# Two weight slots taken per arriving tile of rows in four places, and the key norms' root moved forward

## What is computed

```python
# layer 0: FFN 0, RWKV-7 time mixing, FFN 1; layer 1: FFN 2, short gated convolution, FFN 3
x = x + 0.5 * swiglu(rms(x), w_gu, w_down)         # w_gu 1024 x 5632, w_down 2816 x 1024
r, k, v = xr @ w_r, xk @ w_k, xv @ w_v             # xr, xk, ...: mixtures of a row and the one before
w = decay of (tanh(xw @ w1) @ w2); a = sigmoid(a0 + (xa @ a1) @ a2)
kk = k * k_k, divided per head by max(norm(kk), 1e-12)      # "the key norms"
x = x + o @ w_o                                     # "wo"; o from the recurrence over the tokens
b, c, u = split(rms(x) @ w_in); x = x + (b * conv(c * u)) @ w_out      # "scin", "scout"
```

## Time and profile before

| | |
|---|---|
| median of 3 runs | 1481.89 us (1480.38 to 1483.07) |
| the profiled execution | 1481.93 us, of which the span of the trace is 1480.1 us |
| TensorE busy | 1402.2 us (95%) |
| VectorE, ScalarE, GpSimd busy | 853.8, 584.7, 22.8 us |
| share of the chain that ended last | PE 87%, DVE 5%, ACT 4% |
| granted TensorE clock, mean over the span | 0.965 of full speed |

### The profile page before, as it was taken

One profiled execution on the slowest core, in us unless ns is written; L12 is line 12 of the kernel. 1 busy time (PEld: TensorE's weight loads), 2 busy tenths in 40 slices (PEclk: granted clock), 3 DMA queues, 4 the chain that ended last, 5 costly groups with the idle time before them and its releaser, 6 DMA issues.

```text
span 1480.1 us, 28445 instructions
## 1 busy us (share of the span) xinstructions
PE 1402.2 (95%) x11742; PEld 1359.1 (92%) x11742; DVE 853.8 (58%) x1275; ACT 584.7 (40%) x754; POOL 22.8 (2%) x36
## 2 busy tenths in 40 slices
PE   4999999697799999899999999999999999999997
PEld 4999999586689996699999999999999999999997
DVE  4555544776868254665555455555546766555543
ACT  5333333476344331354333334433333235433332
POOL 0000000300000000200000000000000000000000
PEclk9999999898799797799999999999999999999999
DMA  4433334232135111034433444443444444434342
GB/s 193 151 140 138 137 131 155 86 116 85 60 84 187 36 48 53 29 131 154 142 142 126 147 162 150 154 142 124 139 157 149 147 143 140 167 143 142 128 155 96
DMA packets 44219, 188.97 MB, mean 128 GB/s; under 512 B 15888, under 2 KB 17296, under 8 KB 28016
## 3 DMA queue, kind: packets, MB, share of 16 engines
q1 hardware_dynamic: 44144, 187.89, 36.9%
HBM read 182.65 MB, written 5.22 MB: 127 GB/s over the span
## 4 chain that ended last, share of the span: by engine, by line
PE 87%; DVE 5%; ACT 4%; issue 2%; POOL 1%; DMA 1%; SPq 0%; ACTq 0%; DVEq 0%
PE psum L330 46%; PE psum L362 21%; PE psum L804 5%; PE psum L498 4%; ACT w_hi L243 2%; PE psum L1032 1%; DVE w_lo L248 1%; PE psum L983 1%; PE psum L1052 1%; PE psum L830 1%; PE psum L1001 1%; PE psum L958 1%; PE psum L876 1%; DMA w_raw<-in_gu 1%; PE psum L1048 1%
## 5 line engine op out<-in xcount | busy, mean ns | idle before, releaser
L330 PE MATMUL psum<-x_hi,w_hi 128*128 128x322 f32 (+2 forms) x1600 | 501.4, 313 | 23.5 <-DVE x_lo L295 17.8
L248 DVE TENSOR_TENSOR w_lo<-w_raw,w_hi 128x2048 fp32r<-128x2048 f32 (+1 forms) x188 | 388.2, 2065 | 226.3 <-ACT w_hi L243 225.9
L243 ACT ACTIVATE w_hi<-w_raw 128x2048 fp32r<-128x2048 f32 (+1 forms) x188 | 325.8, 1733 | 459.3 <-PE psum L330 227.2
L330 PE MATMUL psum<-x_lo,w_hi 128*128 128x322 f32 (+2 forms) x1600 | 500.8, 313 | 0.0
L330 PE MATMUL psum<-x_hi,w_lo 128*128 128x322 f32 (+2 forms) x1600 | 499.4, 312 | 0.0
L330 PEld LDWEIGHTS psum<-x_hi,w_hi 128*128 128x128 f32 x1600 | 302.2, 189 | 26.4 <-issue 22.7
L330 PEld LDWEIGHTS psum<-x_hi,w_lo 128*128 128x128 f32 x1600 | 302.9, 189 | 0.0
L330 PEld LDWEIGHTS psum<-x_lo,w_hi 128*128 128x128 f32 x1600 | 302.7, 189 | 0.3
L362 PE MATMUL psum<-h_hi,w_hi 128*128 128x322 f32 (+2 forms) x704 | 219.5, 312 | 0.0
L362 PE MATMUL psum<-h_lo,w_hi 128*128 128x322 f32 (+2 forms) x704 | 219.4, 312 | 0.0
L362 PE MATMUL psum<-h_hi,w_lo 128*128 128x322 f32 (+2 forms) x704 | 219.2, 311 | 0.0
(11 more groups left out here) (200 smaller groups left out, 1394.2 us busy)
## 6 DMA issues: line engine op xcount, KB each, us to landing
w_raw<-in_gu SPq DMA_DIRECT2D x88, 1024.0 KB, 4.7
w_raw<-in_down SPq DMA_DIRECT2D x64, 704.0 KB, 4.1
w_raw<-in_mix SPq DMA_DIRECT2D x16, 1024.0 KB, 4.7
w_raw<-in_scin SPq DMA_DIRECT2D x12, 1024.0 KB, 4.8
w_raw<-in_wo SPq DMA_DIRECT2D x4, 1024.0 KB, 5.5
w_raw<-in_scout SPq DMA_DIRECT2D x4, 1024.0 KB, 4.7
s<-in_wkv SPq DMA_DIRECT2D x8, 256.0 KB, 3.4
out_wkvs<-s SPq DMA_DIRECT2D x8, 256.0 KB, 2.0
```

The costliest lines, as they stand in the source:

```text
L243: act.activation(whi[par][:, :tiles * P], raw[par][:, :tiles * P], ACT.Copy).then_inc(hi_ready, 1)
L248: dve.tensor_tensor(wlo[par][:, :n], raw[par][:, :n], whi[par][:, :n].bitcast(F32), ALU.subtract).then_inc(lo_ready, 1)
L330: last = pe.matmul(PS[:, banks[j], :n], w[:, (2 * k + j) * P:(2 * k + j + 1) * P], v[:, k, :n], start=(k == 0 and i == 0), stop=(k == KT - ...
```

## The change

1. `dual(lag)` orders the tiles of two slots: tile k of slot 0, and from step `lag` on also tile k - lag of slot 1 behind it. It is used in the first feed-forward block (lag 2), for the key projection in the time mixing, and for wo and scout (lag 3 each). The product of one tile moves to `pe_tile`. With lag 2 slot 0 ends after 13 of the 16 tiles, with lag 3 after 12 of 16; before, after 8.
2. In the first feed-forward block `norm_pe` comes after 14 of the 16 tiles.
3. In `project_pe` the waits for the weights of both slots 0 and 1 stand ahead of the first product.
4. In all four feed-forward blocks VectorE makes the `w_lo` that slot 2 needs ahead of the wait for `rstd`, not behind lines 422 and 423.
5. The key norms' bound, root and reciprocal move forward. 
6. Ahead of two of the seven norms (the time mixing's, the final one) ScalarE does an Ln on one column of a constant.

```diff
         def norm_act(act, norm, n):
+            if norm in (1, 6):
+                act.activation(spare[:, 0:1], con[:, K_ONES:K_ONES + 1], ACT.Ln)
             act.wait_ge(ss_done, norm + 1)
...
+        def dual(lag):
+
+            for step in range(KT + lag):
+                if step < KT:
+                    yield 0, step
+                if step >= lag:
+                    yield 1, step - lag
+
+        def pe_tile(pe, par, banks, k, n, xh, xl, shift=0):
+            for j in range(2):
+                for i, (w, v) in enumerate(passes(whi[par], wlo[par], xh, xl)):
+                    last = pe.matmul(PS[:, banks[j], shift:shift + n], w[:, (2 * k + j) * P:(2 * k + j + 1) * P], v[:, k, :n],
+                                     start=(k == 0 and i == 0), stop=(k == KT - 1 and i == 2))
+            return last
...
-            gu_slot(0, 0, fresh=True)
-            norm_pe(pe, {0: 0, 1: 2, 2: 3, 3: 5}[f], 0, n)
-            gu_slot(0, 1)
+            if f == 0:
+                pe_slot_wait(pe, gu)
+                pe.wait_ge(scaled, d["scaled"] + 2)
+                for par, k in dual(2):
+                    if par == 0:
+                        pe.wait_ge(xlo_ready, 8 * d["ver"] + k + 1)
+                    elif k == 0:
+                        pe_slot_wait(pe, gu + 1)
+                    elif k == KT - 2:
+                        norm_pe(pe, 0, 0, n)
+                    last = pe_tile(pe, par, (2 * par, 2 * par + 1), k, n, xhi, xlo)
+                    if k == KT - 1:
+                        last.then_inc(slot_used, 1)
+            else:
+                gu_slot(0, 0, fresh=True)
...
                 if first:
+                    split_dve(dve, gu // 2 + i + 1, par, tiles)
                     norm_dve(dve, {0: 0, 1: 2, 2: 3, 3: 5}[f], n)
...
-                split_dve(dve, gu // 2 + i + 1, par, tiles)
+                if not first:
+                    split_dve(dve, gu // 2 + i + 1, par, tiles)
...
+            pe.wait_ge(scaled, SCALED_BEFORE[name])
+            if name == "wo":
+                pe.wait_ge(mix_evac, MIX_GROUPS - 4)
+            for s in range(2):
                 pe_slot_wait(pe, first + s)
                 pe.wait_ge(x_new, 8 * q + 2 * s - 2)
+            for s, k in dual(3):
                 if s == 0:
...
-            for s in range(4):
-                project(s, XK, s == 0, s == 3, PAD)
+            pe_slot_wait(pe, MIXB)
+            banks = [open_group(), open_group()]
+            for par, k in dual(3):
...
+            act.wait_ge(kk_max, 1)
+            act.activation(tmp[3][0:HEADS, :T], tmp[3][0:HEADS, :T], ACT.Sqrt).then_inc(kk_root, 1)
...
-                if s == 1:
-                    act.wait_ge(kk_max, 1)
-                    act.activation(tmp[3][0:HEADS, :T], tmp[3][0:HEADS, :T], ACT.Sqrt).then_inc(kk_root, 1)
...
+                if k == 3:
+                    dve.wait_ge(kk_root, 1)
+                    dve.reciprocal(rstd[0:HEADS, :], tmp[3][0:HEADS, :T]).then_inc(kk_inv, 1)
...
-            dve.wait_ge(kk_root, 1)
-            dve.reciprocal(rstd[0:HEADS, :], tmp[3][0:HEADS, :T]).then_inc(kk_inv, 1)
```

More of the change, by code:

```diff
@@ L107, in build_program @@
         con = at("con", [P, NCONST])
+        spare = at("spare", [P, 8])
         cin = at("cin", [P, KT * 2 * SEQS])
@@ L345, in ffn_pe @@
                 pe.wait_ge(x_new, 8 * (2 if f == 1 else 5) + 6)
-            gu_slot(0, 0, fresh=True)
-            norm_pe(pe, {0: 0, 1: 2, 2: 3, 3: 5}[f], 0, n)
-            gu_slot(0, 1)
+            if f == 0:
[13 more added lines that the diff above has]
+                gu_slot(0, 0, fresh=True)
+                norm_pe(pe, {0: 0, 1: 2, 2: 3, 3: 5}[f], 0, n)
+                gu_slot(0, 1)
             with pe.Fori(1, FT // 2) as i:
@@ L484, in project_pe @@
             first = stream[name][0]
-            for s in range(4):
+            pe.wait_ge(scaled, SCALED_BEFORE[name])
+            if name == "wo":
+                pe.wait_ge(mix_evac, MIX_GROUPS - 4)
+            for s in range(2):
                 pe_slot_wait(pe, first + s)
                 pe.wait_ge(x_new, 8 * q + 2 * s - 2)
+            for s, k in dual(3):
                 if s == 0:
-                    pe.wait_ge(scaled, SCALED_BEFORE[name])
-                    if name == "wo":
-                        pe.wait_ge(mix_evac, MIX_GROUPS - 4)
+                    pe.wait_ge(olo_ready, olo_base + k + 1)
+                last = pe_tile(pe, s, (2 * s, 2 * s + 1), k, n, ohi, olo)
+                if k == KT - 1:
+                    last.then_inc(slot_used, 1)
+            for s in range(2, 4):
+                pe_slot_wait(pe, first + s)
+                pe.wait_ge(x_new, 8 * q + 2 * s - 2)
                 banks = ((2 * s) % 4, (2 * s + 1) % 4)
                 for k in range(KT):
[L494 to L499, removed]
+                    last = pe_tile(pe, s % 2, banks, k, n, ohi, olo)
                 last.then_inc(slot_used, 1)
@@ L832, in lora_out @@
                     last.then_inc(mix_out, 1)
-            for s in range(4):
-                project(s, XK, s == 0, s == 3, PAD)
+            pe_slot_wait(pe, MIXB)
+            banks = [open_group(), open_group()]
+            for par, k in dual(3):
+                if par == 0:
+                    pe.wait_ge(xlo_ready, 8 * XK + k + 1)
+                elif k == 0:
+                    pe_slot_wait(pe, MIXB + 1)
+                last = pe_tile(pe, par, (banks[par], banks[par] + 1), k, T, xhi, xlo, PAD)
+                if k == KT - 1:
+                    last.then_inc(mix_out, 1)
+            for s in range(2, 4):
+                project(s, XK, False, s == 3, PAD)
             lora_inner(4, XW)
@@ L1421, in mix_dve @@
                 low(XA, k)
+            dve.wait_ge(kk_ss, PAIRS)
+            dve.tensor_scalar(tmp[3][0:HEADS, :T], PS[0:HEADS, 6, :T], 1e-24, None, ALU.max).then_inc(kk_max, 1)
             dve.memset(ar[:, 1, :, 0:PAD], 0.0)
@@ L1432, in mix_dve @@
                     lora_low(1, 1)
-            dve.wait_ge(kk_ss, PAIRS)
-            dve.tensor_scalar(tmp[3][0:HEADS, :T], PS[0:HEADS, 6, :T], 1e-24, None, ALU.max).then_inc(kk_max, 1)
+                if k == 3:
+                    dve.wait_ge(kk_root, 1)
+                    dve.reciprocal(rstd[0:HEADS, :], tmp[3][0:HEADS, :T]).then_inc(kk_inv, 1)
             split(6)
-            dve.wait_ge(kk_root, 1)
-            dve.reciprocal(rstd[0:HEADS, :], tmp[3][0:HEADS, :T]).then_inc(kk_inv, 1)
             split(7)
```

## The result

| | before | changed kernel |
|---|---|---|
| median | 1481.89 us (1480.38 to 1483.18, 5 runs) | 1490.43 us (1485.55 to 1496.71, 5 runs) |
| ratio to before | | 1.0061, 95% interval 1.0038 to 1.0084 |
| the profiled execution | 1481.93 us, span 1480.1 | 1485.55 us, span 1483.8 |
| mean granted TensorE clock of it | 0.965 | 0.963 |

The changed kernel is 0.6% slower, against a forecast of 1488.7 us (+0.46%). The profiled execution was the fastest of its five, so its trace shows only 3.7 us of the 8.5. A second execution (the last experiment) took 1493.42 us.

What follows compares the result with a forecast made beforehand. TensorE, busy 95% of the span, bounds the kernel, so edits count mainly by its waits. +1.65 - 3.7 - 0.7 + 0.1 - 0.75 + 2.1 + 5.3 + 2.8 = +6.8 us gives 1488.7 us, range 1483.0 to 1491.5.

Steps and rivals of the forecast that it cites:

- First block: First feed-forward block: slot 0 ends later, so slot 2 starts at 38.8 instead of 37.15 us, +1.65 us.
- Blocks 2 to 4: Feed-forward blocks two to four: w_lo no longer holds slot 2, which can follow slot 1 at once, together -3.7 us.
- Keys: Key projection in the time mixing: row waits filled, slot 2 held for w_lo, starting at 297.3 against 298.19, -0.9 us.
- Extra Ln: Time mixing's norm and last norm: loads no table earlier, only adds an activation, +0.2 and +0.1 us.
- Key norms: Time mixing: ScalarE 1.3 us ahead, about a quarter of the 2.24 us reciprocal exposed, -0.75 us.
- wo: Output projection wo: no row waits to fill, slot 0 ends later and slot 2 waits until 629.6, +2.1 us.
- scout: Output projection scout: first waits for slot 1's w_lo, 3.1 us, then slot 2 starts at 1226.8, together +5.3 us.
- Clock: First block and scout: long new waits drop TensorE to half clock, 1.4 us each, +2.8; nothing for wo and scout's slot 2 holds.
- more clock: Rival: the holds in wo and scout also let the clock fall, +3.4 us, 1492.1 us; chance 0.1.
- Releases partly hidden: Rival: releases partly hidden, or reciprocal not exposed and keys' slot 2 not held, clock up, 1484.4 us; chance 0.15.
- Faster: Rival: TensorE holds the loop over pairs, so VectorE's 12.0 us of w_hi waits could go, 1477.5 us; chance 0.05.
- Clock stays up: Rival: holds as walked, but clock stays up in the first block and at scout, +4.0 us, 1485.9 us; chance 0.2.

Runs made afterwards that it cites:

- experiment 12: The changed kernel unchanged, measured again as a second set of runs with a second profiled execution: 1487.00 us, ratio 1.0047, +7.0 us.
- experiments 7: The changed kernel with wo and scout put back to the order of before: 1477.33 us, ratio 0.9975, -3.7 us.
- Experiment 4: The changed kernel with the wait for slot 1's weights in wo and scout moved to ahead of slot 1's first tile: 1484.12 us, ratio 1.0019.
- experiment 2: The kernel before with only w_lo made ahead of the wait for rstd in all four feed-forward blocks: 1475.91 us, ratio 0.9963, -5.5 us.
- experiment 6: The kernel before with only the key projection in the new order of slots 0 and 1: 1480.26 us, ratio 0.9993.
- experiment 11: The kernel before with only the extra Ln ahead of the time mixing's norm and the final one: 1480.17 us, ratio 1.0.
- experiment 3: The kernel before with only the key norms' bound, root and reciprocal moved forward: 1480.47 us, ratio 0.9992.
- experiment 9: The kernel before with the new order of slots 0 and 1 in scout only: 1489.54 us, ratio 1.0077, +11.4 us.
- 10: The kernel before with the new order of slots 0 and 1 in wo only: 1485.67 us, ratio 1.0045, +6.7 us.
- experiment 1: The kernel before with the new order of slots 0 and 1 in wo and scout only: 1493.22 us, ratio 1.0069, +10.2 us.

## Why the prediction was right

The forecast of +6.8 us stands just below the two measurements by ratio, +9.0 (5.6 to 12.4) and +7.0 (3.4 to 10.5), and inside both intervals. The time, 1490.43 us, fell in its range, near the upper end. By its own steps:

- **First block, +1.65.** Slot 2 at 38.8 was forecast. It came at 38.30 (+1.15) and 38.93 (+1.78), and at 38.41 and 37.70 in experiments 7 and 4, released by the multiplication by `rstd`, as forecast.
- **Blocks 2 to 4, -3.7.** Slot 2 comes 14.92, 14.83 and 14.84 us after its block's start, where it was 16.12, 16.13 and 15.97: -3.6. The one wait for `w_lo` that is left is scin's. The stages as a whole gained 3.2 us, in experiment 2 without the extra Ln 4.0; the last section has what I know of this difference.
- **Keys, -0.9**: -0.9 (experiment 6, and 18.49 after the first product in the changed kernel). **Extra Ln, +0.2 and +0.1**: 0.11 us at the time mixing's norm and nothing at the last one (experiment 11), and no table load moved.
- **Key norms, -0.75**: -0.9 against the one trace of before, -0.7 against the mean of seven (experiment 3). About a quarter of the reciprocal was to be exposed, 0.56 us. ScalarE waits 0.81 us for the row behind it where it waited 0.34 us before, 0.5 us more.
- **wo, +2.1.** The changed kernel's trace shows only +1.0 (32.42 against 31.39), which would make the term half wrong. The clock hides the rest. The projection starts in a stretch at half clock, and that stretch lasted 6.0 us into wo in the trace of before and 3.4 in the one of after. Two pairs of executions with the same clock from the start of wo to slot 2: 3.5 us at half in experiment 9, where wo is unchanged, gives 15.96 us, and 3.4 in the changed kernel gives 18.04; 6.0 before gives 17.10, and 6.1 in experiment 12 gives 19.23. Both pairs differ by **2.1 us**.
- **scout, +5.3**, 3.1 of them ahead of the first product. That wait cost 3.4 (TensorE starts 5.00 us after scin, not 1.62). From the first product to slot 2 it is 17.60 instead of 14.11, +3.5. The sum, with what the clock takes there, is 6.9; 5.3 + 1.4 = 6.7 was forecast. Experiment 4 takes the first wait away, and the stretch at half clock with it: by the ratios 6.2 us (4.2 against the second set). From the end of scin to block 4 its trace is 3.3 us shorter than that of the changed kernel, although the clock fell behind its hold.
- **Clock, +2.8**, for one stretch each in the first block and at scout. Both are there in both traces of the changed kernel, and the sum counts them about rightly (+0.8 us from slot 2 of the first block to the time mixing, or +1.5 against experiment 11; 1.4 of the 3.5 us in scout). This is still the term that was mis-sized. "So there I count nothing", the prediction said of the 2 us holds in wo and scout. It had set a wait of 2.0 us, behind which the clock fell, against a hold of 1.9 us in scin, behind which it didn't. In the trace of before they read, with a third one that it passed over:

```profile
329.18 0.42 PE L830 MATMUL psum<-t_hi,w_hi 128*128 128x336 f32 x1 [1.86 <-ACT sw L1131]
336.99 0.42 PE L830 MATMUL psum<-t_hi,w_hi 128*128 128x336 f32 x1 [2.23 <-ACT bk L1131]
1134.35 0.42 PE L330 MATMUL psum<-x_hi,w_hi 128*128 128x322 f32 x1 [1.56 <-DVE w_lo L248]
```

The clock fell behind the wait of 1.86 us (at 329.73) and stayed up behind the longer one of 2.23 us (until 343.38). So waits of about 2 us had gone both ways already, and half a chance for each new hold was nearer than none. In the changed kernels the clock fell behind 4 of 10 such holds (scout in experiments 4 and 9, wo in 10 and 12; not in experiment 1, nor in the first trace of after). From slot 2 to the end wo then takes 15.88 instead of 14.38 us, scout 15.7 instead of 14.1: 1.5 each. Two holds at 0.4 chance make 1.2 us. So the rival *more clock* was no rival but a part of the forecast that comes and goes, and moves an execution of the changed kernel by 1.5 or 3 us. That this widens its spread is not shown: it is 11.2 and 10.0 us in its two sets, and up to 10.8 us in those of the kernel before.
- **Rivals.** *Releases partly hidden* fell: all four waits are there, the keys' slot 2 is held by 0.7 us, and a part of the reciprocal is exposed. *Faster* fell: TensorE does not hold the loop over pairs, where VectorE's wait for `w_hi` grew to 14.4 us though TensorE's key slots ended earlier. *Clock stays up* fell with the two stretches.

With the terms as measured the sum is some +7.4 us (first block +1.2, blocks 2 to 4 -3.2, keys with the extra Ln -0.8, norms -0.8, wo +2.1, scout with its clock +6.9, clock in the first block +0.8, behind the two holds +1.2), and no term is off by more than 1.2 us. The total is not right by large errors that cancel.

Two things stay open. By the ratios scout alone (+11.4) and wo alone (+6.7) add up to 18 us, and both together gave 10.2 us, which is apart by more than the intervals. By the medians it is 9.1 + 5.3 = 14.4 against 12.1 us, and that the runs don't tell apart. The stages of the traces allow 9 us without and 13 us with all falls of the clock. What makes wo alone larger than its stage, +3.6 us, was not found. And the small products ahead of wo, which no edit touches, take from 176.8 to 184.8 us in the traces (181.77 before). The mean granted clock of this stretch is 0.89 in the traces in which it takes 176.8 to 177.2 us, and 0.85 to 0.86 in those in which it takes 183.8 to 184.8. Why it differs from execution to execution is open. These 8 us are as much as the kernel before spreads over (7.8 to 10.8 us in its three sets), though it has one trace, and it means that one profiled execution can't price an edit of 3 us unless it is cut by stage.

## What to carry to other kernels

To interleave two slots on the engine that waits is to end the first one later. Where two buffers alternate, ask first what the end of the first slot releases, and how long that chain is; here it was 5 to 6 us with 3 to 4 us of work left to cover it, for 2.7 us saved on the rows, all of it in the first block and the key projection. A wait put ahead of a loop instead of ahead of its use cost 3.4 us and a stretch of half clock. And an operation that needs only an early input (`w_lo`) belongs ahead of a wait for a late one (`rstd`): that one move was worth 5.5 us, more than the other two gains together.

## What was not expected of the hardware

- Holds of the same length, 1.96 to 2.02 us, with TensorE busy throughout on either side, were followed by 3.4 us at half clock four times and by full clock six times. The cost is 1.5 us or nothing.
- The extra Ln alone makes the loops of other stages run differently. From slot 2 of the first block to the time mixing it is 240.88 us with it alone, and 241.6 in the kernels that have neither it nor the first block's new order; blocks 2 and 3 with scin 563.20 against 563.98; block 4 and the end 245.91 against 244.62; scout with the end of scin 29.92 against 29.75. The sum is -0.1 us and the cause is open: the number of products and their waits are the same, and in the second block's down projection the 528 products take 78.32 us against 78.70 without one step above 0.165 us in either.
